# Gate matrix built from high and low parts in 256-column products, with the first attention and its bias table moved earlier

## The chip, the cores and the metric

The kernel runs on one core of one Trainium2 chip. The metric is the time of one execution on the device in microseconds (us); lower is better. The engines are TensorE (PE in the profile; PEld is its weight load), VectorE (DVE), ScalarE (ACT), GpSimd (POOL) and SyncE (SP), which issues transfers.

## The reference

Two transformer blocks over 256 tokens of width 2048, all in float32:

```python
def reference(...):
    x = first_block(...)    # w_in -> 4 branches (pool, SGU, windowed attention, conv)
                            # -> gated merge -> w_out -> layer norm
    return second_block(x)  # SSD + forgetting attention -> w_out -> PEER -> rmsnorm

# sliding_window_attention, in first_block
logits = einsum('bnqhgd,bnkhd->bnhgqk', qb, k_band) * 64 ** -0.5 + band_bias
band_bias = rel_bias[t5_bucket(distance)]          # (16 heads, 128 queries, 256 keys)
probs = softmax(concat([where(mask, logits, -1e30), sink]))[..., :-1]
o = einsum('bnhgqk,bnkhd->bnqhgd', probs, v_band)

# peer, in second_block: 8 heads x 16 of 128*128 experts for each token
idx, g = ...                                       # expert (i1*128+i2) and softmax gate
act = gelu(einsum('thkd,td->thk', u[idx], t))
out = einsum('thk,thkd->td', g * act, v[idx])
```

The kernel computes PEER densely. For each token it builds the gate matrix `[i1, i2]` (sum over its 128 choices of gate times one-hot(i1) times one-hot(i2)), runs all 16,384 experts up, multiplies by the gates, and runs them down.

## The kernel before

All weights come as one stream of blocks of 128 x 2048 floats (1 MB): `ORDER` lists c_kv (blocks 0 and 1), c_q (2 to 9), c_gate (10 to 17), d_val (18 to 25), and so on to 256 expert blocks, 128 up and 128 down. A product of float32 precision is made of three fp32r products. For each block SP loads `raw` (four buffers; the load of block n waits until the low part of block n-4 is made, L365), ACT rounds each half to `whi` (`split_hi`, L378), DVE takes `wlo = raw - whi` (`split_lo`, L384; two buffers of each), and TensorE runs 48 products of 256 columns (`product`, L399 to L401). For up blocks the first two are one product of 512 columns (`product_wide`, L435, L436). ACT and DVE split block n+2 while TensorE works on block n. Each engine's program is written out in order by hand, with semaphores between the engines.

**The bias table.** After block 3, TensorE makes a small product of `relb_sb` and `onehot_b` (L844), whose two loads ACT asks for after its first splits (L1898, L1899). DVE copies the result to `cband` after block 9's work (L1206). POOL, which waits before that for `xlo_ready` and clears a part of `glu` (L752), writes it 128 times per head to HBM (`relative_band`, L755), waits, and reads it back skewed as `cbias` (L758).

**The first attention.** After all eight c_gate blocks TensorE waits until they are evacuated, turns v (L852), waits for `cvtok_ready` and `bias_ready`, and runs `attend_pe`: the scores (L558) with the bias added by a product (L561) for the head pair c = 0, then for each c the turning of the probabilities (L575), the next pair's scores, and a stream block (d_val, d_act) beside each half. `attend_pe` has a hook `lead(i)`, between the first scores and the first turning; here it is empty.

**The gate matrix.** Over up blocks 0 to 53 DVE does the routing in 62 pieces. From up block n = `GATES_FROM` = 58 there are 64 groups of four tokens, eight to each seven blocks (`GATES_FROM + g * 7 // 8 == n`). For a group, DVE makes `one2` (128x512, L1775) and four scaled one-hots `one1` (L1781). Two blocks later TensorE runs four float32 products of 128 columns (L1135; the trace has two records for each) into bank 4 + g % 4, and ACT copies the bank to `gstage` (L2172). POOL stores each eight groups to HBM. The in-order work of ACT and DVE for an up block also has the evacuation (`upart` L2190, `usum` L1814) and the gelu (L2164).

Of the kernel before, what the change touches and what calls it, by code (L numbers as in the profile page):

```python
# [13 lines left out]
T = 256  # L14
# [11 lines left out]
SPLIT = 2  # L26
# [30 lines left out]
GATES_FROM = 58  # L57
# [117 lines left out]
def build(nc, stream, xt, vecs, sgu_wt, sgu_b, relb, buckets, keys, inv_cnt, lnf, out):  # L175
# [12 lines left out]
    def ar(name, shape, kb, dtype=f32):  # L188

        return at(name, shape, ARENA + kb * KB, dtype)  # L190
# [117 lines left out]
    one1 = [ar(f"one1_{i}", [128, 4, 128], 16 + 2 * i) for i in range(4)]  # L308
    one2 = [ar(f"one2_{i}", [128, 4, 128], 96 + 2 * i) for i in range(4)]
# [17 lines left out]
    def bank(i):  # L327
        return pb[i]

    es = ExitStack()  # L330
    with es:
# [345 lines left out]
        def groups_at(n):  # L677

            return [g for g in range(GROUPS) if GATES_FROM + g * 7 // 8 == n]
# [151 lines left out]
        def _(pe):  # L831
            pe.wait_ge(sem("constants"), constant("ones"))
            for _ in range(16):
                nc.tensor.matmul(bank(6)[:, 0:128], ones[:, :], ones[:, :], start=True, stop=True)
            product(pe, Block(0), xhi, xlo, ready=lambda k: pe.wait_ge(sem("xlo_ready"), k // 4 + 1))

            def by_x(b, i, g):
                product(pe, b, xhi, xlo)
            pst = Steps(pe, sem("pe_steps"))
            by_x(Block(1), 0, 0)  # L840
            by_x(Block(2), 0, 0)
            by_x(Block(3), 0, 0)
            pe.wait_ge(sem("onehot_loaded"), 32)
            nc.tensor.matmul(bank(7)[0:16, 0:128], relb_sb[:, :], onehot_b[:, :], start=True,  # L844
                             stop=True).then_inc(sem("band_product"), 1)
# [7 lines left out]
            ins.then_inc(sem("cv_turned"), 1)  # L853
            pe.wait_ge(sem("cvtok_ready"), 1)
# [326 lines left out]
        def _(dve):  # L1181
# [10 lines left out]
            split_lo(dve, Block(0), (0,))  # L1192
            x_lo(1)
# [10 lines left out]
            dve.wait_ge(sem("band_product"), 1)  # L1204
            dve.wait_ge(sem("constants"), constant("band"))
            nc.vector.tensor_copy(cband[:, 128:256], bank(7)[0:16, 0:128]).then_inc(sem("band_ready"), 1)  # L1206
            blocks(dve, st, FIRST["c_gate"], COUNT["c_gate"], lo_only)

            dve.wait_ge(sem("cv_turned"), 1)
# [15 lines left out]
            attend_dve(dve, st, "c", cprob, csmall, co, cgate, True, beside_c)  # L1225
# [538 lines left out]
            def turned_chosen():  # L1764

                dve.wait_ge(sem("chosen_turned"), 1)
                for i in range(3):
                    st.link(nc.vector.tensor_copy(chosenT[i][:, :], bank(4 + i)[:, 0:T]))

            def onehots(g):  # L1770

                o = g % 4
                if g >= 4:
                    dve.wait_ge(sem("gate_product"), g - 3)
                nc.vector.tensor_tensor(  # L1775
                    one2[o][:, :, :], iota[:, :].rearrange("p (a n) -> p a n", a=1).to_broadcast([128, 4, 128]),
                    chosenT[1][:, 4 * g:4 * g + 4].rearrange("p (a n) -> p a n", n=1).to_broadcast([128, 4, 128]),
                    ALU.is_equal)
# [102 lines left out]
        def _(act):  # L1881
            st = Steps(act, sem("act_steps"))

# [14 lines left out]
            act.dma_start(onehot_b[:, :], buckets).then_inc(sem("onehot_loaded"), 16)  # L1898
            act.dma_start(relb_sb[:, :], relb).then_inc(sem("onehot_loaded"), 16)  # L1899
# [34 lines left out]
            run("c_gate", to(cgate, ACT.Silu))  # L1934
# [15 lines left out]
            attend_act(act, "c", cprob, cprobT, csmall, True, beside_c)  # L1950
# [214 lines left out]

            def stage_gates(g):
# [5 lines left out]
                nc.scalar.copy(gstage[half % 2][:, :, 4 * i:4 * i + 4, :],  # L2172
                               bank(4 + g % 4)[:, :].rearrange("p (t e i) -> p e t i", t=4, e=SLICES)
                               ).then_inc(sem("stage_full"), 1)

            for n in range(2 * CHUNKS):
                j = n - CHUNKS + 2
# [25 lines left out]
                for g in groups_at(n - 2):  # L2203
                    stage_gates(g)
# [129 lines left out]
```

## Time and profile before

| | |
|---|---|
| Time, median of 3 runs | 3273.14 us (3272.51 to 3273.68) |
| The profiled execution | 3274.03 us, span 3272.0 us |
| PE busy | 3205.9 us, 98% |
| DVE busy | 2114.4 us, 65% |
| ACT busy | 1558.0 us, 48% |
| Granted TensorE clock, mean | 0.99 of full |
| Share of the chain that ended last | PE 90%, DVE 6%, DMA 2% |
| PE's own longest wait | 11.7 us, for `cbias` (L558) |
| Issue to landing | stream block 4.8 us (median), `relative_band` 36.8 us, `cbias` 19.6 us |
| L1135 (gate products) | x512 records, 66.1 us busy |

A row of a timeline begins with the start and the duration in us; a bracket at its end says how long the engine sat idle before it and what ended that wait. TensorE's records overlap: the pitch from start to start says what a product costs, not the record's length.

### The profile page before, as it was taken

To read this page: it belongs to the slowest core of one execution; us is meant where nothing else is said; L and a number is where in the kernel's file an instruction comes from. 1 tells how busy PE (TensorE), PEld (TensorE's weight loads), DVE (VectorE), ACT (ScalarE), POOL (GpSimd) and SP (SyncE) were. 2 spreads that over 40 slices of the span, in tenths; PEclk is the share of its full clock that TensorE was granted. 3 is DMA by queue.
4 is the path that set the end of the run, shared out by engine and by line. 5 is a ranking of instruction groups with operands and counts; after the bars stand their busy time and mean duration, and the time that the engine had idled before them with its cause. 6 is when DMAs were issued, how large, how long until landed. Compare 5 with 4: busy or idle time off the path is not lost.

```text
span 3272.0 us, 52091 instructions
## 1 busy us (share of the span) xinstructions
PE 3205.9 (98%) x20748; PEld 2928.5 (90%) x20748; DVE 2114.4 (65%) x3315; ACT 1558.0 (48%) x2225; POOL 37.2 (1%) x50
## 2 busy tenths in 40 slices
PE   9899998999999998999999999999999999999998
PEld 9799998999999997999999888888888888888887
DVE  4357977555555567665875789676765566666666
ACT  5455435444444446445554544544444444444444
POOL 0000000000000000000000000000000000000000
PEclk9899999999999998999999999999999999999999
DMA  6634543545555553444354666666667766666664
GB/s 243 185 129 168 181 154 136 193 179 191 181 184 188 202 184 111 151 152 149 122 189 173 198 208 208 212 209 231 218 222 283 253 244 244 244 238 244 244 219 148
DMA packets 108841, 638.86 MB, mean 195 GB/s; under 512 B 11680, under 2 KB 28224, under 8 KB 39792
## 3 DMA queue, kind: packets, MB, share of 16 engines
q1 hardware_dynamic: 100656, 590.92, 51.2%
q0 software_dynamic: 7472, 44.57, 3.9%
q8 instruction: 132, 2.16, 0.3%
q10 hardware_dynamic: 528, 0.78, 0.1%
q14 instruction: 53, 0.43, 0.0%
HBM read 597.42 MB, written 38.80 MB: 194 GB/s over the span
## 4 chain that ended last, share of the span: by engine, by line
PE 90%; DVE 6%; DMA 2%; ACT 1%; issue 1%; SPq 0%; DVEq 0%; ACTq 0%
PE bank L435 22%; PE bank L436 11%; PE bank L399 10%; PE bank L401 10%; PE bank L400 10%; PE bank L1169 7%; PE bank L1167 7%; PE bank L1168 7%; DVE wlo L384 2%; PE bank L1135 2%; DMA relative_band<-cband 1%; PE bank L558 1%; ACT whi L378 1%; PE bank L561 1%; DVE dacc L1244 1%
## 5 line engine op out<-in xcount | busy, mean ns | idle before, releaser
L384 DVE TENSOR_TENSOR wlo<-raw,whi 128x1024 fp32r<-128x1024 f32 x1056 | 1286.4, 1225 | 1056.5 <-ACT whi L378 1053.9
L378 ACT CAST whi<-raw 128x1024 fp32r<-128x1024 f32 x1054 | 1100.2, 1049 | 1137.5 <-PE bank L436 520.8
L435 PE MATMUL bank<-xboth,whi 128*128 128x512 f32 x3072 | 1089.4, 399 | 0.8 <-DVE wlo L384 0.8
L436 PE MATMUL bank<-xboth,wlo 128*128 128x256 f32 x3072 | 860.6, 280 | 0.0
L435 PEld LDWEIGHTS bank<-xboth,whi 128*128 128x128 f32 x3072 | 577.1, 188 | 137.9 <-DVE wlo L384 1.2
L436 PEld LDWEIGHTS bank<-xboth,wlo 128*128 128x128 f32 x3072 | 580.0, 189 | 0.0
L399 PE MATMUL bank<-xboth,whi 128*128 128x256 f32 x1888 | 541.2, 287 | 6.1 <-DVE wlo L384 6.1
L400 PE MATMUL bank<-xboth,whi 128*128 128x256 f32 x1888 | 535.7, 284 | 0.0
L401 PE MATMUL bank<-xboth,wlo 128*128 128x256 f32 x1888 | 535.6, 284 | 0.0
L1167 PE MATMUL bank<-whi,aghi 128*128 128x512 f32 x1024 | 398.4, 389 | 0.0
L1169 PE MATMUL bank<-wlo,aghi 128*128 128x512 f32 x1024 | 398.3, 389 | 0.0
L1168 PE MATMUL bank<-whi,aglo 128*128 128x512 f32 x1024 | 398.3, 389 | 0.0
L399 PEld LDWEIGHTS bank<-xboth,whi 128*128 128x128 f32 x1888 | 363.8, 193 | 7.5 <-issue 3.9
L400 PEld LDWEIGHTS bank<-xboth,whi 128*128 128x128 f32 x1888 | 363.9, 193 | 0.4
L401 PEld LDWEIGHTS bank<-xboth,wlo 128*128 128x128 f32 x1888 | 363.6, 193 | 0.0
L1169 PEld LDWEIGHTS bank<-wlo,aghi 128*128 128x128 f32 x1024 | 192.2, 188 | 40.0
L1168 PEld LDWEIGHTS bank<-whi,aglo 128*128 128x128 f32 x1024 | 192.2, 188 | 39.9
L1167 PEld LDWEIGHTS bank<-whi,aghi 128*128 128x128 f32 x1024 | 192.2, 188 | 39.9
L2182 ACT CAST aghi<-agf 128x256 fp32r<-128x256 f32 x128 | 52.1, 407 | 272.5 <-DVE agf L1795 272.5
L401 PE MATMUL bank<-yhi,wlo 128*128 128x256 f32 x512 | 145.1, 283 | 0.0
L399 PE MATMUL bank<-yhi,whi 128*128 128x256 f32 x512 | 145.0, 283 | 0.0
L400 PE MATMUL bank<-ylo,whi 128*128 128x256 f32 x512 | 145.0, 283 | 0.0
(418 smaller groups left out, 3611.8 us busy)
## 6 DMA issues: line engine op xcount, KB each, us to landing
raw<-stream SPq DMA_DIRECT2D x527, 1024.0 KB, 4.8
up_activations<-ust SPq DMA_DIRECT2D x128, 128.0 KB, 5.1
gate_matrix<-gstage POOLq DMA_DIRECT2D x8, 2048.0 KB, 14.4
gslice<-gate_matrix POOLq DMA_DIRECT2D x8, 2048.0 KB, 10.7
uin<-up_activations SPq DMA_DIRECT2D x32, 512.0 KB, 5.6
relative_band<-cband POOLq DMA_DIRECT2D x1, 3072.0 KB, 36.8
xraw<-xt SPq DMA_DIRECT2D x4, 512.0 KB, 7.8
cbias<-relative_band POOLq DMA_DIRECT2D x1, 2048.0 KB, 19.6
```

The costliest lines, as they stand in the source:

```text
L378: nc.scalar.copy(whi[b.half][:, k, :], raw[b.raw][:, k, :]).then_inc(hi_done, 1)
L384: nc.vector.tensor_tensor(wlo[b.half][:, k, :], raw[b.raw][:, k, :], whi[b.half][:, k, :].bitcast(f32), ALU.subtract).then_inc(lo_done, 1)
L399: nc.tensor.matmul(o, whi[b.half][:, k, :], rhi[:, r, :], start=i == 0, stop=False)
L400: nc.tensor.matmul(o, whi[b.half][:, k, :], rlo[:, r, :], start=False, stop=False)
L401: ins = nc.tensor.matmul(o, wlo[b.half][:, k, :], rhi[:, r, :], start=False, stop=i == len(ks) - 1)
L435: nc.tensor.matmul(o[:, :], whi[b.half][:, k, :], xboth[:, :, k, :], start=k == 0, stop=False)
L436: ins = nc.tensor.matmul(o[:, 0:T], wlo[b.half][:, k, :], xhi[:, k, :], start=False, stop=k == KC - 1)
L1135: ins = nc.tensor.matmul(bank(4 + g % 4)[:, 128 * t:128 * t + 128], one2[g % 4][:, t, :], one1[g % 4][:, t, :], start=True, stop=True)
L1167: nc.tensor.matmul(o[:, :], a_hi[:, tok], v_hi[:, col], start=j == 0, stop=False)
L1168: nc.tensor.matmul(o[:, :], a_lo[:, tok], v_hi[:, col], start=False, stop=False)
L1169: ins = nc.tensor.matmul(o[:, :], a_hi[:, tok], v_lo[:, col], start=False, stop=j == CHUNKS - 1)
L2182: nc.scalar.copy(aghi[j % 3][:, :], agf[j % 3][:, :]).then_inc(sem("ag_hi"), 1)
```

## The change

There are two parts.

1. The gate of a choice is split into `gate_hi` (fp32r) and `gate_lo_part`. A group's product is now four fp32r products of 256 columns: `one2` against high and low one-hots side by side. DVE makes `one2` and a plain one-hot for all four tokens and the scaled high part of two of them; ACT scales the other two high parts and all four low parts (six ACTIVATEs of 128 columns). ACT then stages the high half, and DVE adds the low half to it (`add_low_gates`), between the two halves of its block split. One group goes to each up block, from block 52 on, with two pairs of banks in turn. The 62 pieces of the routing are spread over 48 blocks instead of 54.
2. The two small loads of the bias table are asked first on ACT's queue, the product stands ahead of block 0, and the copy to `cband` behind the first half split of block 0. The first attention begins after block 13: v is turned, blocks 14 and 15 follow, then the first scores, and blocks 16 and 17 are the `lead` of the attention on all three engines.

The core of the diff (buffers and ACT's first-block functions are cut):

```diff
-GATES_FROM = 58
+GATES_FROM = 52
-            return [g for g in range(GROUPS) if GATES_FROM + g * 7 // 8 == n]
+            return [n - GATES_FROM] if 0 <= n - GATES_FROM < GROUPS else []
...
 # TensorE
+            pe.wait_ge(sem("onehot_loaded"), 32)
+            nc.tensor.matmul(bank(7)[0:16, 0:128], relb_sb[:, :], onehot_b[:, :], start=True,
+                             stop=True).then_inc(sem("band_product"), 1)
             product(pe, Block(0), xhi, xlo, ready=lambda k: pe.wait_ge(sem("xlo_ready"), k // 4 + 1))
...
-            blocks(pe, pst, FIRST["c_gate"], COUNT["c_gate"], by_x)
-
-            wait_evacuated(pe, "c_gate")
+            blocks(pe, pst, FIRST["c_gate"], 4, by_x)
+
+            wait_evacuated(pe, "c_q")
...
             ins.then_inc(sem("cv_turned"), 1)
+            by_x(Block(FIRST["c_gate"] + 4), 0, 0)
+            by_x(Block(FIRST["c_gate"] + 5), 0, 0)
...
-                      cprob, cprobT, band, beside_c)
+                      cprob, cprobT, band, beside_c, lambda i: by_x(Block(FIRST["c_gate"] + 6 + i), 0, 0))
...
                 pe.wait_ge(sem("onehots"), g + 1)
-                if g >= 4:
-                    pe.wait_ge(sem("stage_full"), g - 3)
+                pe.wait_ge(sem("gate_scaled"), g + 1)
+                if g >= 2:
+                    pe.wait_ge(sem("stage_full"), g - 1)
                 for t in range(4):
-                    ins = nc.tensor.matmul(bank(4 + g % 4)[:, 128 * t:128 * t + 128], one2[g % 4][:, t, :],
-                                           one1[g % 4][:, t, :], start=True, stop=True)
+                    ins = nc.tensor.matmul(bank(4 + 2 * (g % 2) + t // 2)[:, 256 * (t % 2):256 * (t % 2) + 256],
+                                           one2[g % 4][:, t, :], one1[g % 3][:, t, :, :], start=True, stop=True)
...
 # DVE
             split_lo(dve, Block(0), (0,))
+            dve.wait_ge(sem("band_product"), 1)
+            dve.wait_ge(sem("constants"), constant("band"))
+            nc.vector.tensor_copy(cband[:, 128:256], bank(7)[0:16, 0:128]).then_inc(sem("band_ready"), 1)
...
-                for t in range(4):
+                for t in (2, 3):
                     tok = slice(4 * g + t, 4 * g + t + 1)
-                    ins = nc.vector.tensor_scalar(one1[o][:, t, :], iota[:, :], chosenT[0][:, tok],
-                                                  chosenT[2][:, tok], ALU.is_equal, ALU.mult)
+                    nc.vector.tensor_scalar(one1[g % 3][:, t, 0, :], iota[:, :], chosenT[0][:, tok],
+                                            gate_hi[:, tok].bitcast(f32), ALU.is_equal, ALU.mult)
+                for dst, row in ((one2[g % 4], chosenT[1]), (plain1[g % 3], chosenT[0])):
+                    ins = nc.vector.tensor_tensor(
...
+            def add_low_gates(g):
+
+                half, i = g // 8, g % 8
+                dve.wait_ge(sem("gate_staged"), g + 1)
+                for a in range(2):
+                    rows = gstage[half % 2][:, :, 4 * i + 2 * a:4 * i + 2 * a + 2, :]
+                    low = bank(4 + 2 * (g % 2) + a)[:, :].rearrange("p (t s e i) -> p s e t i", t=2, s=2, e=SLICES)
+                    ins = nc.vector.tensor_tensor(rows, rows, low[:, 1, :, :, :], ALU.add)
+                ins.then_inc(sem("stage_full"), 1)
...
-                    split_lo(dve, Block(UP + n + SPLIT))
+                    split_lo(dve, Block(UP + n + SPLIT), (0,))
+                for g in groups_at(n - 3):
+                    add_low_gates(g)
+                if n + SPLIT < 2 * CHUNKS:
+                    split_lo(dve, Block(UP + n + SPLIT), (1,))
...
 # ACT
+            act.dma_start(onehot_b[:, :], buckets).then_inc(sem("onehot_loaded"), 16)
+            act.dma_start(relb_sb[:, :], relb).then_inc(sem("onehot_loaded"), 16)
...
+            def scale_gates(g):
+
+                act.wait_ge(sem("gate_parts"), 1)
+                act.wait_ge(sem("onehots"), g + 1)
+                if g >= 3:
+                    act.wait_ge(sem("gate_product"), g - 2)
+                for t in range(4):
+                    tok = slice(4 * g + t, 4 * g + t + 1)
+                    if t < 2:
+                        nc.scalar.activation(one1[g % 3][:, t, 0, :], plain1[g % 3][:, t, :], ACT.Copy,
+                                             scale=gate_hi[:, tok].bitcast(f32))
+                    ins = nc.scalar.activation(one1[g % 3][:, t, 1, :], plain1[g % 3][:, t, :], ACT.Copy,
+                                               scale=gate_lo_part[:, tok])
+                ins.then_inc(sem("gate_scaled"), 1)
...
+                for a in range(2):
+                    high = bank(4 + 2 * (g % 2) + a)[:, :].rearrange("p (t s e i) -> p s e t i", t=2, s=2, e=SLICES)
+                    ins = nc.scalar.copy(gstage[half % 2][:, :, 4 * i + 2 * a:4 * i + 2 * a + 2, :], high[:, 0, :, :, :])
+                ins.then_inc(sem("gate_staged"), 1)
 
             for n in range(2 * CHUNKS):
+                for g in groups_at(n - 3):
+                    stage_gates(g)
...
-                for g in groups_at(n - 2):
-                    stage_gates(g)
+                for g in groups_at(n - 1):
+                    scale_gates(g)
```

## Rows read from the trace of the kernel before

**Rows 1.** Timeline of TensorE (start us, us, engine, line, op), 117 to 144 us

```profile
118.00 0.41 PE L852 MATMUL bank<-ident,ckv 128*128 128x128 f32 x2 [1.46 <-issue]
130.06 0.77 PE L558 MATMUL bank<-ckv,cq 128*128 128x128 f32 x2 [11.65 <-DMA cbias<-relative_band]
...
143.31 0.47 PE L399 MATMUL bank<-xboth,whi 128*128 128x256 f32 x1
143.62 0.28 PE L400 MATMUL bank<-xboth,whi 128*128 128x256 f32 x1
143.74 0.29 PE L401 MATMUL bank<-xboth,wlo 128*128 128x256 f32 x1
```

**Rows 2.** Windows, first scores (us busy: PE, PEld, DVE, ACT, POOL; PEclk)

```profile
130.00:135.20 5.20, 5.14 (x16) 4.23 (x16) 0.85 (x3) 1.15 (x1) 0.00 (x0) 0.50 0.01 3
```

**Rows 3.** Timeline of TensorE, the second pair of scores

```profile
157.00 0.39 PE L558 MATMUL bank<-ckv,cq 128*128 128x128 f32 x2
...
159.19 0.59 PE L561 MATMUL bank<-cbias,ident 128*128 128x256 f32 x2
```

**Rows 4.** Timeline of POOL

```profile
73.30 1.26 POOL L755 DMA_DIRECT2D relative_band<-cband  x1 [57.63 <-DVE cband L1206]
```

**Rows 5.** DMA queues, 79 to 81 us (packets, MB, share of 16 engines)

```profile
q0 software_dynamic: 46, 0.21, 100.6%
```

**Rows 6.** DMA queues, 93 to 95 us

```profile
q0 software_dynamic: 42, 0.19, 71.1%
q1 hardware_dynamic: 37, 0.30, 36.1%
```

**Rows 7.** Timelines of SP and ACT

```profile
78.74 0.33 SPq L365 DMA_DIRECT2D raw<-stream  x1
...
100.04 1.28 ACT L378 ACT_TABLE_LOAD   x1 [5.17 <-DMA raw<-stream]
```

**Rows 8.** Timelines of POOL, PE and SP at the start

```profile
15.37 0.30 POOL L752 MEMSET glu<- 128x240 f32 x1 [9.88 <-DVE xboth L1189]
...
17.86 0.39 PE L399 MATMUL bank<-xboth,whi 128*128 128x256 f32 x1 [0.47 <-DVE wlo L384]
...
19.12 0.34 SPq L365 DMA_DIRECT2D raw<-stream  x1
```

**Rows 9.** Timeline of TensorE, two gate groups

```profile
2248.67 1.05 PE L1135 MATMUL bank<-one,one 128*128 128x128 f32 x8
2249.48 0.48 PE L435 MATMUL bank<-xboth,whi 128*128 128x512 f32 x1
...
2255.11 1.05 PE L1135 MATMUL bank<-one,one 128*128 128x128 f32 x8
```

**Rows 10.** Windows in the gate stage

```profile
2240.00:2300.00 60.00, 60.00 (x375) 53.58 (x374) 41.48 (x79) 29.67 (x47) 0.89 (x1) 1.00 0.62 215
```

**Rows 11.** Timelines of DVE and ACT, one gate block

```profile
2251.09 0.42 DVE L1814 TENSOR_TENSOR usum<-bank,upart 128x256 f32<-128x256 f32 x1
2251.42 0.68 DVE L1775 TENSOR_TENSOR one<-iota,chosenT 128x512 f32<-128x512 f32 x1
2252.02 1.11 DVE L1781 TENSOR_SCALAR one<-iota,chosenT,chosenT 128x128 f32<-128x128 f32 x4
...
2250.40 0.58 ACT L2172 COPY gstage<-bank 128x512 f32<-128x512 f32 x1
```

**Rows 12.** Groups of instructions by line (total busy us, mean ns)

```profile
L384 DVE TENSOR_TENSOR wlo<-raw,whi 128x1024 fp32r<-128x1024 f32 x1056 | 1286.4, 1225 | 1056.5 <-ACT whi L378 1053.9 <-ACT whi L1891 1.1
L378 ACT CAST whi<-raw 128x1024 fp32r<-128x1024 f32 x1054 | 1100.2, 1049 | 1137.5 <-PE bank L436 520.8 <-PE bank L401 484.5 <-PE bank L1169 111.5
...
L647 ACT ACTIVATE cprob<-bank,csmall 128x128 f32<-128x128 f32 x16 | 5.9, 368 | 8.9 <-DVE csmall L604 8.9
...
L2139 ACT ACTIVATE last<-x,vec 128x256 fp32r<-128x256 f32 x16 | 7.3, 502 | 16.4 <-DVE x L1573 16.4
```

**Rows 13.** Timeline of DVE in the routing

```profile
2032.55 2.28 DVE L1740 TENSOR_REDUCE chosen<-hit 128x128 f32<-128x2048 f32 x1
```

More of the change, by code:

```diff
@@ L307, in build @@
     chosenT = [ar(f"chosenT{i}", [128, T], 29 + i) for i in range(3)]
-    one1 = [ar(f"one1_{i}", [128, 4, 128], 16 + 2 * i) for i in range(4)]
-    one2 = [ar(f"one2_{i}", [128, 4, 128], 96 + 2 * i) for i in range(4)]
+    one1 = [ar(f"one1_{i}", [128, 4, 2, 128], (16, 20, 24)[i], f32r) for i in range(3)]
+    plain1 = [ar(f"plain1_{i}", [128, 4, 128], 8 + 2 * i) for i in range(3)]
+    one2 = [ar(f"one2_{i}", [128, 4, 128], 96 + 2 * i, f32r) for i in range(4)]
+    gate_hi = ar("gate_hi", [128, T], 31, f32r)
+    gate_lo_part = ar("gate_lo_part", [128, T], 14)
     gstage = [ar(f"gstage{i}", [128, SLICES, 32, 16], 64 - 16 * i) for i in range(2)]
@@ L839, in _ @@
             pst = Steps(pe, sem("pe_steps"))
[L840 to L845, printed above, removed]
+            for n in range(1, 4):
+                by_x(Block(n), 0, 0)
             blocks(pe, pst, 4, FIRST["c_gate"] - 4, by_x)
-            blocks(pe, pst, FIRST["c_gate"], COUNT["c_gate"], by_x)
-            wait_evacuated(pe, "c_gate")
+            blocks(pe, pst, FIRST["c_gate"], 4, by_x)
+            wait_evacuated(pe, "c_q")
             pe.wait_ge(sem("constants"), constant("ident"))
@@ L1203, in _ @@
             blocks(dve, st, FIRST["c_q"], COUNT["c_q"], lo_only)
[L1204 to L1207, printed above, removed]
+            blocks(dve, st, FIRST["c_gate"], 4, lo_only)
+            lo_only(Block(FIRST["c_gate"] + 4), 0, 0)
             dve.wait_ge(sem("cv_turned"), 1)
@@ L1224, in beside_c, with lead_c @@
                 (glu_gate if n >= FIRST["d_act"] else lo_only)(Block(n), 0, 0)
-            attend_dve(dve, st, "c", cprob, csmall, co, cgate, True, beside_c)
+            lo_only(Block(FIRST["c_gate"] + 5), 0, 0)
+            def lead_c():
+                for n in (6, 7):
+                    lo_only(Block(FIRST["c_gate"] + n), 0, 0)
+                wait_evacuated(dve, "c_gate")
+            attend_dve(dve, st, "c", cprob, csmall, co, cgate, True, beside_c, lead_c)
             dve.wait_ge(sem("branch_hi"), branch("hi", "c"))
@@ L1766, in turned_chosen @@
                 dve.wait_ge(sem("chosen_turned"), 1)
-                for i in range(3):
+                for i in range(2):
                     st.link(nc.vector.tensor_copy(chosenT[i][:, :], bank(4 + i)[:, 0:T]))
+                st.link(nc.vector.tensor_copy(gate_hi[:, :], bank(6)[:, 0:T]))
+                nc.vector.tensor_tensor(gate_lo_part[:, :], bank(6)[:, 0:T], gate_hi[:, :].bitcast(f32), ALU.subtract
+                                        ).then_inc(sem("gate_parts"), 1)
             def onehots(g):
-                o = g % 4
@@ L1783, in onehots @@
-                ins.then_inc(sem("onehots"), 1)
+                if g >= 3:
+                    dve.wait_ge(sem("gate_product"), g - 2)
+                    dve.wait_ge(sem("gate_scaled"), g - 2)
+                for t in (2, 3):
+                    tok = slice(4 * g + t, 4 * g + t + 1)
+                    nc.vector.tensor_scalar(one1[g % 3][:, t, 0, :], iota[:, :], chosenT[0][:, tok],
+                                            gate_hi[:, tok].bitcast(f32), ALU.is_equal, ALU.mult)
+                for dst, row in ((one2[g % 4], chosenT[1]), (plain1[g % 3], chosenT[0])):
+                    ins = nc.vector.tensor_tensor(
+                        dst[:, :, :], iota[:, :].rearrange("p (a n) -> p a n", a=1).to_broadcast([128, 4, 128]),
+                        row[:, 4 * g:4 * g + 4].rearrange("p (a n) -> p a n", n=1).to_broadcast([128, 4, 128]),
+                        ALU.is_equal)
@@ L1897, in _ @@
             x_hi(3)
-            act.dma_start(onehot_b[:, :], buckets).then_inc(sem("onehot_loaded"), 16)
-            act.dma_start(relb_sb[:, :], relb).then_inc(sem("onehot_loaded"), 16)
             act.dma_start(vec[:, :], vecs).then_inc(sem("vec_loaded"), 16)
@@ L1933, in _, with gate_out @@
             run("c_q", put_q([cq[:, i, :, :] for i in range(2)]))
-            run("c_gate", to(cgate, ACT.Silu))
+            def gate_out(n):
+                evac(FIRST["c_gate"], to(cgate, ACT.Silu))(Block(FIRST["c_gate"] + n), 0, 0)
+            for n in range(6):
+                gate_out(n)
             act.wait_ge(sem("vec_loaded"), 16)
@@ L1949, in beside_c, with lead_c @@
                     evac(FIRST["d_act"], put_sig(ACT.Sigmoid, 0))(Block(n), 0, 0)
-            attend_act(act, "c", cprob, cprobT, csmall, True, beside_c)
+            def lead_c():
+                for n in (6, 7):
+                    gate_out(n)
+            attend_act(act, "c", cprob, cprobT, csmall, True, beside_c, lead=lead_c)
             act.wait_ge(sem("att_o"), HEADS)
```

10 lines of the change are left out of this document (1 added, 9 removed).

## The prediction

> **What bounds the kernel now.** I read the page's busy shares first, then the waits of TensorE, then the timelines at the three places that the diff touches, then the DMA queues. TensorE is busy 98% of the span and carries 90% of the chain that ended last, so time is won only where TensorE waits or does work that can be shorter, and lost only where a new wait stops it. Its longest wait lies before the first attention: after block 17 it stands 1.46 us, turns v, and stands 11.65 us more until `cbias` has landed [rows 1]. The 5.2 us after that wait run at a granted clock of 0.50, that is 1.2 GHz [rows 2]. In the gate stage it does not wait at all: 60.00 us of 60.00 busy, with DVE at 41.48 and ACT at 29.67 [rows 10]. There the question is how long TensorE's own work is, and whether DVE and ACT, which get more to do, still fit beside it.
>
> **First attention.** Block 17's modelled end is 118.00 - 1.46 = 116.54, and block 18 starts at 143.31: 26.8 us [rows 1]. The work in it is two pairs of scores at 157.00 to 159.19 + 0.43 = 2.62 us each at full clock [rows 3], and eight turnings of 128 columns, an estimate of 0.9 us from the 0.41 us of two [rows 1]: 6.2 us. After the change blocks 14 and 15 cover the copy of `cvtok`, and blocks 16 and 17 (5.76 us each, 48 products at the pitch 143.62 to 143.74 = 0.12 us [rows 1]) cover maxima, exponentials and scaling of c = 0. So the idle time, the half clock and the stand before the first turning go: **-20.6 us**. For that the table must be there at the first scores. TensorE reaches them at about 17.86 + 15 x 5.76 = 104.3 us [rows 8]. The whole way from the store's issue to the scores takes 130.06 - 73.30 = 56.8 us [rows 1, 4]. POOL's earlier work ends at 15.67 [rows 8], so the store begins near 15.7 instead of 73.3, and the table lands near 72.5, with 32 us to spare. That margin is the cover; behind the wait everything of TensorE would stand. ACT gets two more switches between the tables of Silu and Exp, inside blocks 14 to 18, where it is half idle: nothing.
>
> **The start.** The two small loads go ahead of ACT's first rounding, which waits for x anyway; the tiny product and the copy to `cband` lie beside the loads of x and block 0. The copy puts some 0.3 us into DVE's chain of x parts, which TensorE follows at half clock with more distance than that: nothing. What I do charge is the collision. The 3 MB store in small pieces now runs while the ring of raw blocks fills. Between 79 and 81 us the store's queue held the 16 engines to 100.6% at 0.21 MB in 2 us, and the stream got nothing [rows 5], though a load was issued at 78.74; it landed at about 100.0, when ACT's wait of 5.17 us for it ended [rows 7]. Later the two shared, packet for packet (42 and 37), with 0.30 MB for the stream in 2 us, or 7.0 us for a block [rows 6]. TensorE never stopped there, because the ring was full.
>
> Now the ring is not full. Block 5 starts near 17.86 + 4 x 5.76 = 40.9 us [rows 8], and its raw must land 1.05 + 1.23 + 0.1 = 2.4 us earlier [rows 12], at 38.5. Its load is issued at 19.12, 3.4 us after the store [rows 8]. The bounds:
> - Below: from the start the queues share packet for packet. The loads of 3, 4 and 5 are then out together and come about 7 us apart, 5 at about 38, and 6, 7 and 8 each some 1 us later than needed until the store ends near 52.5: a loss of 0 to 1 us.
> - Middle: the load of 5 meets the fate of the load of 78.74, which landed 26.7 us after the store's issue: 15.7 + 26.7 = 42.4, or 3.9 us late, and about 1 us of half clock behind the gap.
> - Above: it is besides behind one more block at the shared rate, 7.0 us: 10.9 us late, with the 2.6 us that 5.2 us of half clock cost [rows 2]: 13.5 us.
>
> I take the middle, **+5 us**, as the nearest row has it.
>
> The Trainium skill (DMA: Bandwidth & Descriptors, section "Queues, rings and completion order") says that each DMA engine goes round robin between the queues that have work, at the granularity of a packet. By that rule the lower bound would hold and the sum would be 5 us less; the shared stretch agrees with it (42 to 37 packets) and the stretch from 79 to 81 us does not (46 to 0).
>
> **The gate products.** A group takes TensorE from 2248.67 to 2249.48 = 0.81 us [rows 9]. Four fp32r products of 256 columns, each with its own weights as in L399 to L401, have a pitch of 0.12 [rows 1]: 0.48 us. 64 x 0.33 = **-21.1 us**. Bounds: -24 if leaving the float32 form gives 0.05 us a group besides (an estimate from the record after the group, 0.48 us long [rows 9]); nothing or less if the others can't follow. A block with its group takes 2255.11 - 2248.67 = 6.44 us now [rows 9], and would take 6.11.
> - DVE per block: 41.48 / 60 x 6.44 = 4.45 us [rows 10]. Of the four scaled one-hots (1.11) two go (-0.55), `plain1` is another 128x512 (+0.68), and the two additions of 256 columns are like L1814 (+0.84) [rows 11]: 5.4 us of 6.11. If each addition cost as much as 512 columns, 5.9. It fits.
> - ACT per block: 29.67 / 60 x 6.44 = 3.18 [rows 10]. The copy of 0.58 [rows 11] becomes two halves, 0.8 together (bounds 0.58 and 1.16), and six ACTIVATEs of 128 columns with an operand for each partition come in, 0.37 each by L647 [rows 12]: 2.2. Sum 5.6 of 6.11. Above, with L2139's 0.50 (scaled, written as fp32r, but twice the columns) [rows 12] and 1.16: 6.8.
> - The order: behind ACT's second rounding of a block stand the evacuation, the gelu, the scaling and the staging; the first half of the next rounding comes last, about 5.7 us after the block's end. DVE's low half and the addition follow, and TensorE needs them a whole block later. `gate_scaled` comes some 1.5 us before TensorE asks. So no new wait ends last.
> - Starting 6 blocks earlier costs TensorE nothing. Stores and slices of the gate matrix end three blocks later than before, with some seven blocks left.
>
> **The routing** is pressed into 48 blocks: 62 / 48 = 1.29 pieces for each. The dearest are 12 of 2.28 us [rows 13]: DVE then has 2 x 1.23 + 0.42 + 1.29 x 2.28 = 5.8 us in a block of 6.44 - 0.81 = 5.6. Over the nine blocks of these pieces it falls back 1.8 us at most, which the lead of two split blocks takes up: 0, bound 1.8.
>
> **Sum.** 3274.0 (the profiled execution; its span is 3272.0) - 20.6 - 21.1 + 5 = 3237.3. The median of the runs lies 0.9 below that execution: **3236.4 us**.
>
> **The rivals.**
> - *Fair sharing at the start.* No loss there: 3231 us. For it: the even packets of rows 6, and that three loads are already out when the store begins. Against: rows 5. Chance 0.27.
> - *Strong starvation.* The loss is 9 to 13.5 us: 3240 to 3245 us. For it: nothing of the stream moved in rows 5, and more loads are outstanding than at 73.3. Against: a load issued ahead of the store was not slowed there. Chance 0.22.
> - *ACT or DVE bounds a part of the gate stage.* At a period of 6.3 us, 9 us of the 21 are left: 3248 us. For it: ACT's upper price. Against: L647 is the nearer shape. Chance 0.10.
> - *Slower: ACT bounds the gate stage outright.* If the six ACTIVATEs cost 0.50 each and the halves 0.58 each, ACT needs 6.76 us for a block against 6.44 now: 64 x 0.32 = 20.5 us lost instead of 21.1 won, 3278 us. The rest of the change gives 15.6 us, so this decides from a period of 6.44 + 15.6 / 64 = 6.68 us. Chance 0.03.
> - *No change.* The same mechanism at just about 6.68 us, or a table that for all its 32 us of margin is still awaited, so that the first part does nothing it says, with a dear start. Chance 0.01.
> - My forecast, with a loss of 1 to 9 us at the start: 0.37, with a range of its own of 3231 to 3241.
>
> About 0.2% (6.5 us) is what a measurement of this kernel can tell from no change. Every case but the last two is faster by more: 0.96, then 0.01 and 0.03. The range goes from fair sharing with the -24 for the gates (3228, and 1 for the roundings) to the strong start together with half of the gates' gain (3236.4 + 8.5 + 10.5 = 3255): 3227 to 3255.
>
> **What would show it.** In the profile after: no wait of L558 for `cbias`, and the first scores before block 16. `relative_band` issued near 15.7, with the waits of TensorE for `wlo` between 35 and 65 us summing to 4 us (0: fair sharing; over 8: starvation) and a granted clock under 1 there. In the gate stage a period of 6.1 us, TensorE still at 100%, L1135 with 256 records or so, DVE near 0.88 and ACT near 0.9 of the stretch. A period above 6.2 with waits for `one` or `whi` would prove the gate part wrong, as would idle time of TensorE between 1950 and 2070 us the routing.

## The result and the profile after

The changed kernel takes 3231.47 us, median of four runs (3230.19 to 3233.67), against 3272.92 us (3272.51 to 3273.68) for the kernel before on the same chip: ratio 0.9873, 95% interval 0.986 to 0.9885. That is 41.5 us less. The forecast was 3236.4 us, so the kernel gained 4.9 us more than I had worked out. The profiled execution took 3232.62 us with a span of 3230.6 us, 41.4 us less than the span before.

Head of the page of the changed kernel, and its two rows on the bias table:

```profile
span 3230.6 us, 52168 instructions
## 1 busy us (share of the span) xinstructions
PE 3179.6 (98%) x20492; PEld 2901.3 (90%) x20492; DVE 2163.3 (67%) x3380; ACT 1664.2 (52%) x2672; POOL 37.3 (1%) x50
...
relative_band<-cband POOLq DMA_DIRECT2D x1, 3072.0 KB, 38.2
...
cbias<-relative_band POOLq DMA_DIRECT2D x1, 2048.0 KB, 19.5
```

TensorE is still busy for 98% of a shorter span. Its waits over the whole span (us in total, times, longest):

```profile
PE bank L421 <- DVE first L1448: 8.3, 1, 8.3
PE bank L402 <- DVE wlo L387: 7.7, 8, 3.5
```

The wait of 11.65 us for `cbias` [rows 1] no longer appears among them. POOL's timeline says why (the store of the band, then the load of the table; an idle time and its releaser stand in brackets):

```profile
15.36 0.30 POOL L755 MEMSET glu<- 128x240 f32 x1 [9.87 <-DVE xboth L1194]
15.61 1.26 POOL L758 DMA_DIRECT2D relative_band<-cband  x1
54.13 1.20 POOL L761 DMA_DIRECT2D cbias<-relative_band  x1 [37.27 <-DMA relative_band<-cband]
```

The store goes out at 15.61, not at 73.30 [rows 4]. The table lands at 54.13 + 19.5 = 73.6, and TensorE asks for it at 105.57. The margin is 32 us, as forecast. Timeline of TensorE there: first and last product of the first scores, the start of block 16, the first turning, and the start of block 18:

```profile
105.57 0.39 PE L561 MATMUL bank<-ckv,cq 128*128 128x128 f32 x2
...
107.76 0.59 PE L564 MATMUL bank<-cbias,ident 128*128 128x256 f32 x2
108.01 0.47 PE L402 MATMUL bank<-xboth,whi 128*128 128x256 f32 x1
...
119.71 0.82 PE L578 MATMUL bank<-ident,cprob 128*128 128x128 f32 x6
...
122.80 0.47 PE L402 MATMUL bank<-xboth,whi 128*128 128x256 f32 x1
```

The pair of scores lasts 108.01 - 105.57 = 2.44 us, at full clock, and no row has a wait in front. The first turning follows block 17 directly. Block 18 starts at 122.80, where it was 143.31 [rows 1]: 20.5 us earlier, with whatever the start lost already taken off. The remaining 20.9 us of the span come behind it: the up blocks with the gate groups are 21.7 us shorter (from the last product of L1071, now L1075, to the last of L435, now L438: 2566.3 - 1651.0 = 915.3 us before, 2525.0 - 1631.4 = 893.6 now), and what lies between block 18 and there is 0.9 longer, as executions differ there (the second trace of the changed kernel, below, is another 1.6 longer). Two gate groups of the changed kernel on TensorE, and the windows of 100 us around them (us busy of PE, PEld, DVE, ACT, POOL; PEclk; DMA share; GB/s):

```profile
2204.89 0.64 PE L1140 MATMUL bank<-one,one 128*128 128x256 f32 x4
2205.36 0.40 PE L438 MATMUL bank<-xboth,whi 128*128 128x512 f32 x1
...
2211.01 0.65 PE L1140 MATMUL bank<-one,one 128*128 128x256 f32 x4
```

```profile
2200.00:2300.00 100.00, 100.00 (x589) 87.83 (x589) 84.54 (x148) 79.81 (x201) 1.77 (x2) 1.00 0.67 232
```

A group now takes 2205.36 - 2204.89 = 0.47 us, not 0.81, and the period is 2211.01 - 2204.89 = 6.12 us, not 6.44 [rows 9]. 64 x 0.34 = 21.8 us are the 21.7. TensorE stays at 100 of 100 us; DVE stands at 0.85 and ACT at 0.80 of the stretch, so neither bounds it.

What is left is the start, where I had charged 5 us. Waits of TensorE between 17 and 60 us:

```profile
PE bank L402 <- DVE wlo L387: 1.2, 2, 0.8
```

One of the two, 0.38 us, is that of block 1 at 17.80, which the kernel before has too (0.47 [rows 8]). The other, 0.85 us at 53.46, before block 7, is new: that is the collision, and it is not 5 us. Block 1 starts at 17.80 and the first scores at 105.57, 87.8 us later. The queues between 27 and 29 us (packets, MB, share of 16 engines), and ACT's rounding of blocks 5, 6 and 7, whose wait ends when their raw block lands:

```profile
q0 software_dynamic: 44, 0.20, 71.3%
q1 hardware_dynamic: 39, 0.29, 34.9%
```

```profile
36.83 2.00 ACT L381 CAST whi<-raw 128x1024 fp32r<-128x1024 f32 x2 [5.50 <-DMA raw<-stream]
...
43.91 2.00 ACT L381 CAST whi<-raw 128x1024 fp32r<-128x1024 f32 x2 [4.30 <-DMA raw<-stream]
...
51.01 2.00 ACT L381 CAST whi<-raw 128x1024 fp32r<-128x1024 f32 x2 [4.30 <-DMA raw<-stream]
```

The store's queue and the stream move nearly as many packets as each other, as in [rows 6], and the blocks land 7.1 us apart. Block 5 lands at 36.8. I had forecast 42.4, needed 38.5, and put the rival of fair sharing at "about 38".

### The profile page after: what moved, and what is told of

Same layout as the page of the kernel before. It is cut to its first block, busy times and chain, and to the rows that moved or that the text cites. A ratio compares the mean times of both kernels' runs of the same rounds, so it can differ in the third digit from the quotient of the medians.

```text
span 3230.6 us, 52168 instructions
## 1 busy us (share of the span) xinstructions
PE 3179.6 (98%) x20492; PEld 2901.3 (90%) x20492; DVE 2163.3 (67%) x3380; ACT 1664.2 (52%) x2672; POOL 37.3 (1%) x50
## 4 chain that ended last, share of the span: by engine, by line
PE 91%; DVE 6%; DMA 1%; ACT 1%; issue 1%; SPq 0%; DVEq 0%; ACTq 0%
PE bank L438 22%; PE bank L439 11%; PE bank L402 10%; PE bank L404 10%; PE bank L403 10%; PE bank L1172 7%; PE bank L1173 7%; PE bank L1174 7%; DVE wlo L387 2%; DMA raw<-stream 1%; PE bank L1140 1%; ACT whi L381 1%; PE bank L564 1%; PE bank L561 1%; DVE dacc L1256 1%
## 5 line engine op out<-in xcount | busy, mean ns | idle before, releaser
L438 PE MATMUL bank<-xboth,whi 128*128 128x512 f32 x3072 | 1089.6, 399 | 0.9 <-DVE wlo L387 0.9
L438 PEld LDWEIGHTS bank<-xboth,whi 128*128 128x128 f32 x3072 | 577.3, 188 | 140.2 <-DVE wlo L387 1.2
## 6 DMA issues: line engine op xcount, KB each, us to landing
cbias<-relative_band POOLq DMA_DIRECT2D x1, 2048.0 KB, 19.5
```

Source lines behind the costliest of these rows:

```text
L438: nc.tensor.matmul(o[:, :], whi[b.half][:, k, :], xboth[:, :, k, :], start=k == 0, stop=False)
```

## The experiments

Two theories were open after the result. *Additive*: the two parts of the change are independent, each is worth its own term (about 21 us each), and the start costs 0 to 1 us because the queues share. *Other*: the gate part is worth more or less than its term, and the difference hides in the first part, or the start does cost 5 us and something else gives them back.

**The gate part alone.** The kernel before with the hunks of the gate part only; of these:

```diff
-GATES_FROM = 58
+GATES_FROM = 52
...
-                    ins = nc.tensor.matmul(bank(4 + g % 4)[:, 128 * t:128 * t + 128], one2[g % 4][:, t, :],
-                                           one1[g % 4][:, t, :], start=True, stop=True)
+                    ins = nc.tensor.matmul(bank(4 + 2 * (g % 2) + t // 2)[:, 256 * (t % 2):256 * (t % 2) + 256],
+                                           one2[g % 4][:, t, :], one1[g % 3][:, t, :, :], start=True, stop=True)
```

> The kernel before with the gate part alone: split gates, 256-column products, one group to each up block from block 52; first attention and bias table as before. If a group costs 0.48 us instead of 0.81, as its trace and the pitch of 0.12 us say, 64 groups give 21 us: 3252 us, with an up-block period of 6.12 us in the gate stage. Rival (the gain of the whole comes mostly from the first part): under 10 us gained, 3263 us or more.

Measured: 3251.27 us (3250.33 to 3251.99), ratio 0.9934 (0.9917 to 0.9951), 21.8 us under the 3273.05 of the kernel before beside it. TensorE's timeline:

```profile
2253.23 0.65 PE L1139 MATMUL bank<-one,one 128*128 128x256 f32 x4
...
2259.36 0.64 PE L1139 MATMUL bank<-one,one 128*128 128x256 f32 x4
```

The period is 6.13 us, as in the whole change. The term of -21.1 holds; 21.8 is 64 x 0.34.

**The first part alone.** The kernel before with the other hunks; of these:

```diff
-            blocks(pe, pst, FIRST["c_gate"], COUNT["c_gate"], by_x)
+            blocks(pe, pst, FIRST["c_gate"], 4, by_x)
...
+            by_x(Block(FIRST["c_gate"] + 4), 0, 0)
+            by_x(Block(FIRST["c_gate"] + 5), 0, 0)
...
-                      cprob, cprobT, band, beside_c)
+                      cprob, cprobT, band, beside_c, lambda i: by_x(Block(FIRST["c_gate"] + 6 + i), 0, 0))
```

> The kernel before with the first part alone: table asked first, attention begun among the c_gate blocks; gates as before. If 20.6 us of waits and half clock go and the start loses about 1 us: 3253 us. The two parts then add up to the whole within 1 us. Rival (the parts share a gain, through the clock or the transfers): the sum of the two gains differs from the whole by over 3 us.

Measured: 3253.30 us (3251.10 to 3257.09), ratio 0.9943 (0.9927 to 0.996), 19.8 us less. The two halves make 21.8 + 19.8 = 41.6 us, and the whole makes 41.5. That they agree to 0.1 us is luck: the four runs here spread over 6 us, and their interval goes from 13 to 24 us less. The sum shows that the parts are additive to a few us, and can't price the start. The trace can: TensorE is busy for 30.00 of 30.00 us between 35 and 65, and it gets from block 1 (17.37) to the first scores (104.07) in 86.7 us. The store is issued as in the whole change, and the start loses nothing.

**The table early, the attention where it was.** The changed kernel with the first attention put back behind all eight blocks of `c_gate`, on all three engines:

```diff
-            blocks(pe, pst, FIRST["c_gate"], 4, by_x)
+            blocks(pe, pst, FIRST["c_gate"], COUNT["c_gate"], by_x)
...
-            by_x(Block(FIRST["c_gate"] + 4), 0, 0)
-            by_x(Block(FIRST["c_gate"] + 5), 0, 0)
```

> The changed kernel with the first attention back behind all eight c_gate blocks and no lead; the table still asked first. If two waits are removed by two edits, the wait for the table (11.7 us) and its half clock go here, but TensorE still stands for the evacuation, the copy of v and the softmax of the first head pair, some 6 to 8 us in pieces: 3238 to 3240 us. Rival (the early table does it all): 3232 us.

Measured: 3240.92 us (3238.34 to 3241.54), ratio 0.99 (0.9883 to 0.9916), 9.4 us above the whole change, 0.9 us past the 3240 that I gave as the upper end. A wait of TensorE that the whole change does not have, its timeline before the first scores, and windows (0.50 is PEclk) behind these stands:

```profile
PE bank L578 <- DVE cprob L621: 3.6, 1, 3.6
```

```profile
117.36 0.41 PE L854 MATMUL bank<-ident,ckv 128*128 128x128 f32 x2 [1.46 <-issue]
118.69 0.80 PE L561 MATMUL bank<-ckv,cq 128*128 128x128 f32 x2 [0.92 <-DVE cvtok L1214]
```

```profile
118.60:121.40 2.80, 2.71 (x8) 2.37 (x9) 0.03 (x1) 0.00 (x0) 0.00 (x0) 0.50 0.73 202
126.60:131.00 4.40, 4.38 (x16) 3.68 (x17) 0.74 (x4) 0.96 (x2) 0.00 (x0) 0.50 0.00 0
```

The waits are 3.6 + 1.46 + 0.92 = 6.0 us. The other 3.4 us are half clock: the granted clock is 0.50 (1.2 GHz) in both windows, after TensorE had stood, and half of their 2.80 + 4.40 = 7.2 us is 3.6. So the blocks laid between the steps of the attention are worth about 9.4 us, of which a third is clock.

**The attention early, the table late.** The changed kernel with the small loads, the tiny product and the copy to `cband` back in their old places:

```diff
-            act.dma_start(onehot_b[:, :], buckets).then_inc(sem("onehot_loaded"), 16)
-            act.dma_start(relb_sb[:, :], relb).then_inc(sem("onehot_loaded"), 16)
...
+            dve.wait_ge(sem("band_product"), 1)
+            dve.wait_ge(sem("constants"), constant("band"))
+            nc.vector.tensor_copy(cband[:, 128:256], bank(7)[0:16, 0:128]).then_inc(sem("band_ready"), 1)
```

> The changed kernel with the bias table asked, multiplied and copied where it was before; attention still begun after block 15. The table lands near 130 us and the first scores now stand before it from 104 us on, 26 us, with two blocks of work behind them that were before it: 8 us worse than before in this stretch, so 3274 - 21 + 8 = 3260 us. Rival (the lead alone hides most of the wait): 3240 us or less.

Measured: 3252.87 us (3252.32 to 3257.19), ratio 0.9943 (0.9926 to 0.9959): 21.4 us above the whole change and 7 us under what I expected. TensorE and POOL:

```profile
124.15 0.76 PE L561 MATMUL bank<-ckv,cq 128*128 128x128 f32 x2 [19.05 <-DMA cbias<-relative_band]
```

```profile
73.17 1.26 POOL L758 DMA_DIRECT2D relative_band<-cband  x1 [57.65 <-DVE cband L1211]
109.72 1.20 POOL L761 DMA_DIRECT2D cbias<-relative_band  x1 [35.30 <-DMA relative_band<-cband]
```

The wait is there, 19.05 us of it, as it must be if the early table is what removes it. My miss is that I took the table's landing from before (130.06 [rows 1]). It now landed at 124.15, because the load of `cbias` took 124.15 - 109.72 = 14.4 us against 19.5 in the changed kernel. While TensorE stands, no raw buffer comes free, so the stream soon asks for nothing: from 120 to 124 us its queue moved 1 packet and the table's 244, where the kernel before, whose TensorE began to stand 13 us later, had 174 and 175 between 120 and 125. Here a transfer that everything waited for was sped up by the wait.

**The store earlier.** The changed kernel with the store ahead of POOL's `glu` memset, which waits for the last x part:

```diff
-            pool.wait_ge(sem("xlo_ready"), 4)
-            nc.gpsimd.memset(glu[:, :, 0:CONV_K - 1], 0.0).then_inc(sem("constants"), 1)
-
             pool.wait_ge(sem("band_ready"), 1)
             pool.dma_start(band_d, ...)
+
+            pool.wait_ge(sem("xlo_ready"), 4)
+            nc.gpsimd.memset(glu[:, :, 0:CONV_K - 1], 0.0).then_inc(sem("constants"), 1)
```

> The changed kernel with POOL issuing the store of the table before it clears its part of glu, near 10 us instead of 15.6. If queues that both hold work share the engines packet for packet, a block of the stream comes each 7.0 us from about 14 us on while the store lasts, instead of each 5.76 that TensorE needs; with fewer blocks ahead the waits of TensorE for wlo in the first 60 us grow from 1 us to about 5 us: 3236 us. Rival (the store takes the engines for itself as between 79 and 92 us of the kernel before): a wait of over 10 us in one piece, 3245 us.

Measured: 3233.67 us (3232.82 to 3237.10), ratio 0.9882 (0.9866 to 0.9899). The store goes out at 10.39 instead of 15.61, and TensorE's waits from 17 to 60 us are:

```profile
PE bank L402 <- DVE wlo L387: 3.0, 4, 1.0
```

3.0 us for 1.2, and 2.2 us on the median. The first scores come 107.37 - 17.75 = 89.6 us after the start of block 1, for 87.8 in the changed kernel's trace and 86.7 in its second one (below). The direction is as expected, the size half of it, and the ranges of the two kernels overlap (3230.19 to 3233.67, and from 3232.82). Even a store that is under way while x still loads does not starve the ring.

**The store once the ring is full.** The changed kernel with one more wait on POOL, so that the store goes out at 43.57:

```diff
             pool.wait_ge(sem("band_ready"), 1)
+            pool.wait_ge(lo_done, 14)
```

> The changed kernel with POOL's store of the table waiting until block 6 is split, near 44 us, where the ring of raw blocks is full and one load at a time is asked. The table lands near 101 us, 3 us before the scores need it. If a load that is asked after the store's pieces are queued stands behind them (as the one of 78.74 did), the loads asked behind the store take 18 to 22 us here too, where those that were out before it alternated with it in the changed kernel; the full ring covers it: no wait of TensorE, 3231 us, within 1.5 us of the changed kernel. Rival (the queues always alternate and the stretch of 79 to 91 us was an accident): loads take 7 to 12 us each.

Measured: 3232.08 us (3230.80 to 3235.01), ratio 0.9877 (0.9861 to 0.9894): no difference from the changed kernel, as expected. Its queues are the reason to show it. First 48 to 50 us, then 50 to 60 us; the stream's queue has no row in either:

```profile
q0 software_dynamic: 47, 0.22, 99.9%
...
q0 software_dynamic: 218, 1.00, 96.4%
```

The load of 43.04 had landed after 4.9 us, so the store had the engines alone when the next load was asked at 48.80. That load got no packet before 60 us and landed at 70.6, when ACT's wait for it ended:

```profile
70.60 2.00 ACT L381 CAST whi<-raw 128x1024 fp32r<-128x1024 f32 x2 [5.15 <-DMA raw<-stream]
```

So the monopoly of [rows 5] is real and comes back on demand. The two runs above whose stores go out near 73 us, the gate part alone and the late table, have it as well: 221 packets to none between 79 and 89 us. It hits a load that is asked while the store runs alone.

**ACT scales all eight parts.** The changed kernel with DVE's two scaled one-hots given to ACT:

```diff
-                for t in (2, 3):
-                    tok = slice(4 * g + t, 4 * g + t + 1)
-                    nc.vector.tensor_scalar(one1[g % 3][:, t, 0, :], iota[:, :], chosenT[0][:, tok],
-                                            gate_hi[:, tok].bitcast(f32), ALU.is_equal, ALU.mult)
...
-                    if t < 2:
-                        nc.scalar.activation(one1[g % 3][:, t, 0, :], plain1[g % 3][:, t, :], ACT.Copy,
-                                             scale=gate_hi[:, tok].bitcast(f32))
+                    nc.scalar.activation(one1[g % 3][:, t, 0, :], plain1[g % 3][:, t, :], ACT.Copy,
+                                         scale=gate_hi[:, tok].bitcast(f32))
```

> The changed kernel with ACT scaling all eight parts of a group, DVE none. ACT's chain for a block grows by 2 x 0.29 from 4.9 us to 5.5 us, still under the period of 6.12: no change, 3232 us. Rival (ACT or the order of its work already sets the period): 0.6 us a block, 38 us slower.

Measured: 3233.54 us (3231.71 to 3234.37), ratio 0.9878 (0.9862 to 0.9894), within the spread of the changed kernel. Windows of the same 100 us:

```profile
2200.00:2300.00 100.00, 100.00 (x589) 87.86 (x588) 74.93 (x117) 89.53 (x231) 1.77 (x2) 1.00 0.67 234
```

ACT rises from 79.81 to 89.53, DVE falls from 84.54 to 74.93, and TensorE does not notice.

**ACT past its limit.** As the last, with each of the eight parts scaled in two ACTIVATEs of 64 columns:

```diff
+                    for h in (slice(0, 64), slice(64, 128)):
+                        nc.scalar.activation(one1[g % 3][:, t, 0, h], plain1[g % 3][:, t, h], ACT.Copy,
+                                             scale=gate_hi[:, tok].bitcast(f32))
+                        ins = nc.scalar.activation(one1[g % 3][:, t, 1, h], plain1[g % 3][:, t, h], ACT.Copy,
+                                                   scale=gate_lo_part[:, tok])
```

> The same with each of the eight parts scaled in two ACTIVATEs of 64 columns, about 0.24 us each: ACT's chain for a block becomes 4.9 - 1.8 + 3.9 = 7.0 us and sets the period. If the slower rival of the prediction is right in its price, the gate stage now has a period of 7.0 us, 64 x 0.9 = 56 us above the changed kernel: 3288 us, slower than before. Rival (the split blocks ahead soak it up): under 3250 us.

Measured: 3275.90 us (3275.01 to 3278.79), ratio 1.0011 (1.0001 to 1.0021), 44.4 us above the whole change. Windows, and two groups on TensorE:

```profile
2200.00:2300.00 100.00, 92.07 (x526) 77.83 (x525) 65.43 (x101) 100.00 (x321) 0.89 (x1) 1.00 0.59 206
```

```profile
2304.87 0.71 PE L1140 MATMUL bank<-one,one 128*128 128x256 f32 x4 [0.50 <-issue]
...
2311.74 0.71 PE L1140 MATMUL bank<-one,one 128*128 128x256 f32 x4 [0.61 <-issue]
```

Now ACT has 100 of 100 us and TensorE 92. The period is 2311.74 - 2304.87 = 6.87 us, where I had expected 7.0. From the first group to the last it is 2511.2 - 2079.0 = 432.2 us, and 2468.7 - 2082.4 = 386.3 in the changed kernel: 45.9 us over 63 periods, 6.86 for each, so the lead of the split blocks hides less than 1 us. In this trace the first group also comes 3.4 us earlier, ahead of anything that the edit touches. That is a difference between executions; with differences of that size 45.9 and the 44.4 of the medians agree. The whole gain of the change is gone at this period. My slower rival said it would be from 6.68.

**High part only.** The changed kernel without the low halves of the gates: TensorE's products have 128 columns, ACT scales two parts, and DVE adds nothing.

```diff
-                    ins = nc.tensor.matmul(bank(4 + 2 * (g % 2) + t // 2)[:, 256 * (t % 2):256 * (t % 2) + 256],
-                                           one2[g % 4][:, t, :], one1[g % 3][:, t, :, :], start=True, stop=True)
+                    ins = nc.tensor.matmul(bank(4 + 2 * (g % 2) + t // 2)[:, 256 * (t % 2):256 * (t % 2) + 128],
+                                           one2[g % 4][:, t, :], one1[g % 3][:, t, 0, :], start=True, stop=True)
...
-                for g in groups_at(n - 3):
-                    add_low_gates(g)
```

> The changed kernel without the low parts of the gates: products of 128 columns over the high parts only, ACT scales two parts instead of six, DVE adds nothing; the low half of every gate is left out of the result. It prices a product: if its cost goes with the columns, a group falls from 0.48 to 0.24 us and the time by 15 us, to 3217 us. Rival (the weight load sets a floor near 0.1 us for each product, as the pitch of the float32 records of 128 columns does): 0.4 us for a group, 5 us less, 3227 us.

> The changed kernel itself, on the chip of the run with high parts only, for the comparison: 3231.5 us, with 1 us of waits for wlo after block 1 in the first 60 us.

Measured: 3227.28 us (3225.01 to 3228.20), ratio 0.9859 (0.9842 to 0.9875), against 3232.43 us (3229.77 to 3233.95), ratio 0.9872 (0.9855 to 0.9888), for the changed kernel once more on the same chip. One group:

```profile
2200.56 0.56 PE L1140 MATMUL bank<-one,one 128*128 128x128 f32 x4
2200.96 0.45 PE L438 MATMUL bank<-xboth,whi 128*128 128x512 f32 x1
```

The group takes 0.40 us: half the columns save only 0.07 of 0.47 us. From the first group to the last it is 2460.9 - 2079.6 = 381.3 us for 386.3. A cost that goes by columns would have given 0.24 us and about 3217 us. So a product of 128 columns with weights of its own costs 0.10 us, and one of 256 costs 0.12. That is where the change's gain comes from: the second 128 columns of a 256-column product are nearly free, while the float32 form paid 0.81 / 4 = 0.20 us for 128. That form has eight records for a group [rows 9], again 0.10 us each. By these prices fp32r products of 128 columns, eight for a group, would take 0.80 us (an estimate), and so no less than before: what pays is to have four products for eight. That form was not run.

The second trace of the changed kernel also answers for the start. Its waits of TensorE between 17 and 60 us:

```profile
PE bank L402 <- DVE wlo L387: 0.4, 1, 0.4
```

This is the wait of block 1, at 17.78. I had expected 1 us behind it, and there is none. The first scores come 104.49 - 17.78 = 86.7 us after block 1. Six kept traces with the store issued as in the changed kernel (this one, the first part alone, the table early, both ACT runs, high part only) have TensorE busy for 30.00 of 30.00 us between 35 and 65. Only the first trace of the changed kernel has the wait of 0.85 us.

No version that computes the whole gate matrix was faster than the changed kernel by more than its runs differ.

## Why the prediction was right, and where it was off

**First attention, -20.6.** Right, and 0.9 too small. From block 1 to block 18 it was 143.31 - 17.86 = 125.5 us. It is 105.0 in the first trace of the changed kernel, with the start's 1.1 us in it, and 103.9 in the second trace and in that of the first part alone: 21.5 us less. The two mechanisms I named are separately shown: without the early table 19.05 us of wait come back, and without the blocks between the steps 9.4 us.

**The start, +5.** This is the term that was mis-sized: it measured 0 to 1.1 us, 1.1 in the first trace of the changed kernel (87.8 us from block 1 to the first scores for 86.7, with one wait of 0.85) and nothing in the second. The mechanism I described exists, but I applied it to the wrong state of the queues. I took the load of 78.74 as the nearest row [rows 7] and gave its fate to the load of 19.07. In the kernel before, and again with the store at 43.57, the store's first packets came between 77.0 and 77.5 and between 47.0 and 47.5 us, the stream's only load landed within a microsecond of them (72.97 + 5.0 and 43.04 + 4.9), and the next load had to get in behind the store. In the changed kernel the ring was being filled: the stream had loads outstanding when the store's first packets came, at 20 us, and all through it, and the two shared from then on (398 packets of the stream to 409 between 25 and 45 us). The loads asked at 21.70 and 26.33, behind the store too, did not starve. So it is not the order of asking. I had written that down as what spoke for the rival ("three loads are already out when the store begins") and weighed it too low. The lower bound, a loss of 0 to 1 us, was the right value. With it the sum is 3231.4 to 3232.4, and the rival of fair sharing said 3231. So the result lies in my range, but the case that came true is this rival's, with 0.27, and not my own, with 0.37. My sign for it was 0 us of waits for `wlo` between 35 and 65 us, and the two traces of the changed kernel have 0.8 and 0.

The Trainium skill (DMA: Bandwidth & Descriptors, section "Queues, rings and completion order") has each DMA engine go round robin between queues with work, a packet at a time. The changed kernel's trace, where both queues had work when the store began, agrees (44 packets to 39); the run with the store at 43.57 does not, with 218 packets to none over 10 us while a load was outstanding. The rule gave the better forecast here. All four traces in which the store began as the stream's last outstanding load landed break it, and all eight in which it began beside several loads keep it; that this is the cause is read from them and not shown otherwise. Why the second queue is shut out, and why it gets its turn again after some 13 us, stays open.

**The gate products, -21.1.** Right: 0.47 us for a group against 0.48 forecast, a period of 6.12 against 6.11, -21.7 in the trace and -21.8 alone. The bound of -24, for something saved beside the group, has nothing behind it.

**ACT and DVE beside it.** Both fit, as said. DVE's 0.85 of the stretch is 5.2 us a block (5.4 forecast) and ACT's 0.80 is 4.9 (5.6 forecast). Most of ACT's difference is that I summed durations where the engine overlaps its instructions. Its timeline:

```profile
2206.63 0.39 ACT L2213 ACTIVATE one<-plain,gate_hi 128x128 fp32r<-128x128 f32 x1
2206.92 0.39 ACT L2215 ACTIVATE one<-plain,gate_lo_part 128x128 fp32r<-128x128 f32 x1
...
2208.39 0.62 ACT L2227 COPY gstage<-bank 128x256 f32<-128x256 f32 x2
2208.90 1.05 ACT L381 CAST whi<-raw 128x1024 fp32r<-128x1024 f32 x1
2211.21 1.05 ACT L381 CAST whi<-raw 128x1024 fp32r<-128x1024 f32 x1 [1.26 <-PE bank L439]
```

Each ACTIVATE lasts 0.39 us but the next starts 0.29 us later, so six cost 1.8 us and not 2.2; the two halves take 0.6 and not 0.8. ACT still idles 1.26 us in each block, waiting for TensorE. That is its distance from being the bound. The Trainium skill (ScalarE: Activation LUTs, section "What ACT_TABLE_LOAD costs") gives 186 ns and 0.833 ns for each column, about 93 ns more for an operand with one value for each partition, and an overlap of about 93 ns between ACTIVATEs back to back. An estimate from it for 128 columns is 0.386 us and a pitch of 0.29 us. The rows agree, with 0.39 and 0.29.

**The rivals.** Fair sharing came true. Strong starvation fell: behind block 1 the start has one wait, of 0.85 us, in one trace. That ACT bounds a part, or all, fell with its 1.26 us idle in each block, though the run with sixteen ACTIVATEs shows that the mechanism and its price were drawn rightly. The routing cost nothing: TensorE is busy for 120.00 of 120.00 us between 1950 and 2070.

## What to carry to other kernels

When a big transfer is moved next to a stream, don't price it by a row of the same transfer in another place until you have asked which queue will have work outstanding when it starts: the same 3 MB store shared evenly with a stream that was filling its ring, and shut it out for over 10 us when the ring was full and nothing was outstanding. TensorE lost next to nothing in either case, because the full ring covers the gap; ask that as well. Then sum an engine's work by the distance between starts, not by durations, and look at what it idles in a block to see how far it is from being the bound. For products with weights of their own, fill 256 columns: the second 128 cost 0.02 us here. And before a loss of 1 us is called measured, read the same stretch in every trace that has it: here one of seven showed it.

## What was unexpected in the hardware

- A load asked while a large store has the DMA engines to itself got no packet for over 10 us (218 to 0 between 50 and 60 us) and landed after 22 us, where 4.9 us is usual. Loads already outstanding at the store's start share with it.
- The fp32r product of 128 columns with new weights has a pitch of 0.10 us, against 0.12 for 256 columns.
- The load of `cbias` took 14.4 us where the stream fell silent during it, and 19.5 us beside the stream.
- The clock granted to TensorE while block 0 runs (9 to 14 us) is 0.67 in the changed kernel's profile, 0.73 in its second one, 0.66 in that of the kernel before and 1.00 in that of the gate part alone. It can make little of the 3.5 us by which runs of one kernel differ: block 1 starts at 17.80, 17.78, 17.86 and 17.49. What sets it was not tried.
